# Decoder block on one core: where VectorE computes the convolution's 31 taps

## The chip, the cores and the metric

The kernel runs on one core of one Trainium2 chip. The metric is the device time of one execution in microseconds (us), the median of several runs; a second look comes from one profiled execution, whose span and rows are in us from its first instruction.

## The reference, cut to what matters

One decoder block on 256 tokens of width 1024, all in float32: a causal depthwise convolution branch and an attention branch run on the same projections, are gated and mixed, and a mixture of 32 experts (4 for each token) follows.

```python
u = rms_norm(h, norm1_g)
proj = u @ w_in                       # conv a, g (512 each), q, k, v (512 each), gates (2048)
# convolution branch
hc = a * sigmoid(g)
hc = depthwise_conv(hc, conv_dw, width 31, causal) + dw_b     # 512 channels
y_conv = silu(layer_norm(hc)) @ w_conv_out
# attention branch: 8 heads of 64, causal, ALiBi, q and k normed per head
y_attn = softmax(q k^T * scale - slope * distance) v @ w_attn_out
mixed = sigmoid(gate1) * y_conv + sigmoid(gate2) * y_attn
h = h + mixed @ w_out
u2 = rms_norm(h, norm2_g)
# top 4 of 32 experts, clamped SwiGLU, 2048-wide up/gate, 1024-wide down
h = h + moe_ffn(u2, w_router, w_up_gate, w_down, ...)
```

## The kernel before

The program is written by hand for each engine (`@block.sync`, `.scalar`, `.vector`, `.tensor`, `.gpsimd`); each engine executes its own list in order, and semaphores order the engines among one another. Nothing is scheduled by a tool: what stands ahead on an engine's list runs ahead.

**Dense stage.** The 1024x4608 projection is cut into nine groups of 512 columns: 0 and 1 are the convolution's two halves, 2, 3 and 4 are q, k and v, 5 to 8 are the gates. A dense product is made of three products (`product3`, L1038): every operand is split into a high part, rounded, and a low part, the difference. For weights, ScalarE writes the high part (`weights_high(i, b)`, L499, into `w_hi`) and VectorE the low part (`weights_low(i, b)`, L698, into `w_lo`), in two halves `b` for each group `i`. VectorE's `weights_low` waits for ScalarE's high part.

**Convolution.** The 31 taps are VectorE's (`taps(first, end)`). A round is one tap for all 512 channels: four instructions of 128x256, one for each block of 128 channels. Round 0 is at L720, the others at L723. A tap adds to the same accumulator `cv`, so each waits for the same channel block's tap of the round before. The last one raises `cv_done`. In the trace `hp` and `cv` are named `up_odd`, since they lie in the buffer of that expert's weights. Rounds 0 to 7 (`early_taps = 8`) stand ahead of the attention heads, among the low parts; the other 23 are dealt out over the eight heads, two or three to each:

```python
taps(*[early_taps + (TAPS - early_taps) * (h + i) // HEADS for i in range(2)])
```

**Attention on VectorE.** First `rqk` (L738) and the scaling of q and k (L744), then the four copies of q and k transposed (L752), then the loop over heads: a head adds the distance term to the scores (L766), takes the row maxima (L769, L770), their negative (L771, `nmx_ready`), then the reciprocal of the sums of the head before (L777, `rsm_ready`), then its taps; behind the taps of heads 2, 3, 5 and 7 stands a half of `weights_low(7)` or `weights_low(8)`, and behind those of heads 4, 6 a low part of the attention output (`attention_low`, L756).

**Attention on TensorE.** Groups 5 to 8 are 16 pieces of 24 matmuls (L1038); behind piece i stands `between(i)`: the transposes of q and k (L1130) at i = 1, the scores of head i-2 (L1103, L1104), the transposes of the probabilities of head i-5 (L1111), the product with v of head i-6 (L1121 to L1123), and at i = 11 the sum over channels for the convolution's layer norm (L1010), ahead of which TensorE waits for `cv_done`. The transposes of head g's probabilities need ScalarE's scaling, and that needs `rsm_ready` of head g, which VectorE raises in its piece for head g+1. The product with v of heads 2, 4 and 6 needs `attention_low` of the pair before.

**Behind it.** The layer norm, its sigmoid, the attention and convolution output products, mixing and `w_out` follow on the same chain, then the router, then one loop over tiles of tokens, expert by expert. The 32 experts' weights (12.6 MB each) stream through two sets of buffers, all on SyncE's queue. The first loads stand behind events of the dense stage: a part of expert 1's up weights behind `pv_done` of the last head, two behind the convolution's low part (`cv_lo`), others behind the mixing and `w_out`.

Of the kernel before, what the change touches and what calls it, by code (L numbers as in the profile page):

```python
# [56 lines left out]
def hybrid_block(nc, x, norm1_g, w_in, b_gates, conv_dw, conv_dw_b, conv_ln_g, conv_ln_b, w_conv_out,  # L57
# [3 lines left out]
    with ctx:  # L61
# [219 lines left out]
        def w_parts(i):  # L281
            k = stream[i][1].shape[1]
            return [t[:, :].rearrange("p (k n) -> p k n", k=k) for t in (w_hi[i % 2], w_lo[i % 3])]

        def half_cols(w, b):
            n = w.shape[2] // 2
            return w[:, :, b * n:(b + 1) * n]
# [371 lines left out]
        def _(dve):  # L659
            steps = [0]  # L660

            def done(ins):
                steps[0] += 1
                ins.then_inc(dve_step, 1)
                return steps[0]
# [29 lines left out]
            def weights_low(i, b):  # L695
                hi, lo = w_parts(i)
                dve.wait_ge(w_hi_ready, 2 * (i - 1) + b + 1)
                nc.vector.tensor_tensor(half_cols(lo, b), half_cols(stream[i][1], b), half_cols(hi, b).bitcast(F32),  # L698
                                        ALU.subtract).then_inc(w_lo_ready, 1)
# [15 lines left out]
            def taps(first, end):  # L715
                for w in range(first, end):
                    for c in range(KC):
                        tap = hp[:, c, w:w + T]
                        if w == 0:
                            landed[c] = done(nc.vector.tensor_scalar(cv[:, c, :], tap, dwT[:, c, 0:1], dwb[:, c:c + 1], ALU.mult, ALU.add))  # L720
                        else:
                            dve.wait_ge(dve_step, landed[c])
                            ins = nc.vector.scalar_tensor_tensor(cv[:, c, :], tap, dwT[:, c, w:w + 1], cv[:, c, :], ALU.mult, ALU.add)  # L723
                            if w == TAPS - 1 and c == KC - 1:
                                ins.then_inc(cv_done, 1)
                            else:
                                landed[c] = done(ins)

            early_taps = 8
            taps(0, 4)  # L730
            for b in range(2):
                weights_low(4, b)
            taps(4, early_taps)
            for b in range(2):
                weights_low(5, b)

# [4 lines left out]
            for i, t in enumerate((qn, kn)):  # L741
                v = t.rearrange("p m (h d) -> p (m h) d", d=HD)
                f = rqk[:, i * 16:i * 16 + 16].unsqueeze(2).to_broadcast([P, 16, HD])
                nc.vector.tensor_tensor(v, v, f, ALU.mult).then_inc(qk_scaled, 1)  # L744
            for b in range(2):
                weights_low(6, b)


            for j in range(4):
                i, m = divmod(j, 2)  # L750
                dve.wait_ge(qkT_full, j + 1)
                nc.vector.tensor_scalar((qT, kT)[i][:, :, m * P:(m + 1) * P], bank[4 + j][:].rearrange("p (a b) -> p a b", a=4),  # L752
                                        (qg, kg)[i], None, ALU.mult).then_inc(qkT_ready, 1)
            def attention_low(c):
                dve.wait_ge(o_hi, c + 1)
                nc.vector.tensor_tensor(ao_r[1][:, c, :], O_BANK[:, 0:T], ao_r[0][:, c, :].bitcast(F32), ALU.subtract).then_inc(o_read, 1)  # L756


            for h in range(HEADS + 1):
                if h < HEADS:  # L760
                    s = sc[h % 3]
                    slope = 2.0 ** (-8.0 * (h + 1) / HEADS)
                    dve.wait_ge(s_full, h + 1)
                    if h >= 3:
                        dve.wait_ge(t_full, h - 2)
                    nc.vector.scalar_tensor_tensor(s, dist, -slope * HD ** 0.5, S_BANKS[h % 2][:, 0:384],  # L766
                                                   ALU.mult, ALU.add).then_inc(s_read, 1)
                    dve.wait_ge(s_read, h + 1)
                    done(nc.vector.reduce_max(mx[:, h % 2, 0:1], s[:, 0:P], AX.X))  # L769
                    step(nc.vector.reduce_max(mx[:, h % 2, 1:2], s[:, P:3 * P], AX.X))  # L770
                    nc.vector.tensor_scalar(nmx[:, h % 2, :], mx[:, h % 2, :], -HD ** -0.5, None, ALU.mult).then_inc(nmx_ready, 1)  # L771
                if h >= 1:
                    g = h - 1
                    dve.wait_ge(exp_done, 2 * h)
                    if g >= 2:
                        dve.wait_ge(p_scaled, 2 * g - 2)
                    nc.vector.reciprocal(rsm[:, g % 2, :], sm[:, g % 2, :]).then_inc(rsm_ready, 1)  # L777
                if h < HEADS:
                    taps(*[early_taps + (TAPS - early_taps) * (h + i) // HEADS for i in range(2)])
                if h in (2, 3, 5, 7):  # L780
                    b = (2, 3, 5, 7).index(h)
                    weights_low(7 + b // 2, b % 2)
                if h >= 4 and h % 2 == 0:
                    attention_low((h - 4) // 2)
# [5 lines left out]
            freed(dve, U_MEAN)  # L790
            nc.vector.tensor_tensor(sq, xc, xc, ALU.mult).then_inc(sqr_ready, 1)
            attention_low(3)
            for b in range(2):
                weights_low(ATT_W, b)
# [598 lines left out]
```

## Time and profile before

| | us |
|---|---|
| median of 3 runs | 1136.68 |
| lowest, highest | 1135.35, 1137.06 |
| the profiled execution | 1133.76 |
| its span, first to last instruction | 1132.0 |
| TensorE busy in it | 970.9 |
| VectorE busy in it | 394.3 |
| ScalarE busy in it | 310.1 |
| HBM read | 431.59 MB |

The profiled execution lies 2.92 us below the median of the timed runs and 1.59 us below the lowest. In the rows a group of instructions is named by engine and line: PE is TensorE's matmuls, PEld its weight loads, DVE VectorE, ACT ScalarE, SPq SyncE's queue of transfers. The idle time in square brackets is that ahead of the instruction, with the engine and line whose work ended it. Two instructions of one engine can overlap by some 0.08 us in the rows, so what one more instruction costs is taken from start to start and not from the duration of one.

### The profile page before, as it was taken

The numbers are of one execution on the slowest core, as the hardware profiler recorded it, in microseconds if no ns is written. First come the engines' busy times: TensorE is split into PE (matmuls) and PEld (weight loads), VectorE is DVE, ScalarE is ACT, GpSimd is POOL, SyncE is SP. The second block draws the span as 40 slices with busy tenths as digits, with TensorE's granted clock in tenths as the row PEclk, the third lists the DMA queues.
The fourth block names the chain that finished last, engine by engine and source line by source line (L and its number), as shares of the span: only waits on it lengthen the run. The fifth ranks groups of instructions, "written<-read, shape, count | busy, mean of one in ns | idle before, by whom it ended". The sixth has DMA issues, their size and how long they took to land.

```text
span 1132.0 us, 19760 instructions
## 1 busy us (share of the span) xinstructions
PE 970.9 (86%) x7261; PEld 446.7 (39%) x7262; DVE 394.3 (35%) x1014; ACT 310.1 (27%) x534; POOL 5.3 (0%) x27
## 2 busy tenths in 40 slices
PE   6999698998766668889996799998997966998677
PEld 5998598732212113223331233332332321332122
DVE  4689968432111112222331133332332321232111
ACT  4565474122111111212222022331331311232111
POOL 1000000000000000000000000000000000000000
PEclk8999899999898888999998799999998999999888
DMA  7573068999999999999999999999999999999996
GB/s 268 178 278 138 12 223 354 402 406 425 426 430 426 426 426 427 426 426 426 426 426 426 426 426 426 426 425 424 427 426 426 427 426 426 426 428 426 426 427 252
DMA packets 50918, 432.97 MB, mean 382 GB/s; under 512 B 4845, under 2 KB 5265, under 8 KB 18128
## 3 DMA queue, kind: packets, MB, share of 16 engines
q1 hardware_dynamic: 50424, 432.50, 91.7%
q8 instruction: 16, 0.26, 0.1%
q10 hardware_dynamic: 472, 0.16, 0.1%
q14 instruction: 6, 0.05, 0.0%
HBM read 431.59 MB, written 1.05 MB: 382 GB/s over the span
## 4 chain that ended last, share of the span: by engine, by line
PE 48%; DMA 24%; SPq 20%; DVE 5%; issue 2%; ACT 1%; DVEq 0%; ACTq 0%
PE bank L1307 15%; SPq L404 12%; DMA up_odd<-in_w_up_gate 10%; DMA up_even<-in_w_up_gate 10%; PE bank L1038 9%; PE bank L1341 8%; SPq L410 6%; PE bank L1229 5%; DMA down_even<-in_w_down 3%; DVE up_odd L723 3%; PE bank L1298 3%; PE bank L1276 2%; PE bank L1068 1%; PE bank L1327 1%; DVE w_lo L698 1%
## 5 line engine op out<-in xcount | busy, mean ns | idle before, releaser
L1307 PE MATMUL bank<-up_even,reg_r 128*32 128x512 f32 x1472 | 187.2, 653 | 69.1 <-DMA up_even<-in_w_up_gate 69.1
L1307 PE MATMUL bank<-up_odd,reg_r 128*32 128x512 f32 x1408 | 186.2, 675 | 62.0 <-DMA up_odd<-in_w_up_gate 62.0
L993 DVE TENSOR_TENSOR ys<-reg_m,ys 64x512 fp32r<-64x512 f32 x90 | 61.7, 685 | 236.0 <-ACT ys L650 235.4
L1307 PEld LDWEIGHTS bank<-up_even,reg_r 128*32 128x32 f32 x1472 | 46.9, 115 | 202.0 <-DMA up_even<-in_w_up_gate 102.4
L1307 PEld LDWEIGHTS bank<-up_odd,reg_r 128*32 128x32 f32 x1408 | 45.6, 117 | 194.7 <-issue 97.4
L638 ACT ACTIVATE reg_m<-reg_m 128x256 f32<-128x256 f32 x45 | 18.9, 419 | 371.1 <-DVE reg_m L974 371.1
L1229 PE MATMUL bank<-reg_h,reg_r 128*32 128x256 f32 x736 | 93.2, 636 | 0.7 <-DVE reg_r L864 0.7
L974 DVE TENSOR_SCALAR reg_m<-bank 128x256 f32<-128x256 f32 x45 | 19.1, 425 | 212.4 <-PE bank L1307 212.4
L1341 PE MATMUL bank<-down_even,reg_r 128*32 128x512 f32 x736 | 84.4, 596 | 0.4 <-DMA down_even<-in_w_down 0.2
L646 ACT ACTIVATE reg_m<-bank,gslot 128x512 f32<-128x512 f32 x45 | 31.0, 688 | 194.8 <-PE bank L1341 194.8
L1341 PE MATMUL bank<-down_odd,reg_r 128*32 128x512 f32 x704 | 80.3, 595 | 0.1
L934 DVE TENSOR_TENSOR reg_r<-bank,g2c 128x256 f32<-128x256 f32 x46 | 19.5, 424 | 129.3 <-PE bank L1235 129.3
L638 ACT ACT_TABLE_LOAD x45 | 57.7, 1283 | 5.5 <-DVE cum L957 4.7
L650 ACT ACTIVATE ys<-reg_m 64x512 fp32r<-64x512 f32 x90 | 56.6, 629 | 2.0
L1298 PE MATMUL bank<-ys,hotT 128*128 128x512 f32 x184 | 56.9, 432 | 0.0
L630 ACT ACTIVATE reg_r<-bank 128x256 f32<-128x256 f32 x46 | 17.7, 384 | 131.7 <-PE bank L1229 131.7
L1298 PEld LDWEIGHTS bank<-ys,hotT 128*128 128x128 f32 x184 | 32.6, 198 | 51.2 <-issue 46.1
L723 DVE SCALAR_TENSOR_TENSOR up_odd<-up_odd,reg_m 128x256 f32<-128x256 f32 x120 | 48.3, 478 | 0.0
L1038 PE MATMUL bank<-u_hi,w_hi 128*128 128x256 f32 x160 | 48.2, 301 | 0.0
L1276 PE MATMUL bank<-bup,sel 128*128 128x512 f32 x92 | 47.2, 595 | 0.0
L1038 PE MATMUL bank<-u_lo,w_hi 128*128 128x256 f32 x160 | 46.4, 290 | 0.0
L1038 PE MATMUL bank<-u_hi,w_lo 128*128 128x256 f32 x160 | 46.3, 289 | 0.0
(252 smaller groups left out, 1185.7 us busy)
## 6 DMA issues: line engine op xcount, KB each, us to landing
up_even<-in_w_up_gate SPq DMA_DIRECT2D x64, 2048.0 KB, 36.4
up_odd<-in_w_up_gate SPq DMA_DIRECT2D x64, 2048.0 KB, 38.4
down_even<-in_w_down SPq DMA_DIRECT2D x64, 1024.0 KB, 36.5
down_odd<-in_w_down SPq DMA_DIRECT2D x64, 1024.0 KB, 36.5
down_even<-in_w_in SPq DMA_DIRECT2D x6, 2048.0 KB, 8.4
down_odd<-in_w_in SPq DMA_DIRECT2D x2, 2048.0 KB, 8.7
down_odd<-in_w_in SPq DMA_DIRECT2D x4, 512.0 KB, 8.9
down_odd<-in_w_attn_out SPq DMA_DIRECT2D x1, 2048.0 KB, 7.4
```

The lines of the kernel that those rows point to most:

```text
L404: sp.dma_start(up_part(a, c), w_up_gate[bass.ds(e, 1), :, :].rearrange("e (p k) n -> p (e k n)", k=KD)[:, n * c:n * c + n]).then_inc(up_in ...
L410: sp.dma_start(down_part(a, c), w_down[bass.ds(e, 1), 2 * c * P:(2 * c + 2) * P, :].rearrange("e (p r) n -> p (e r n)", r=2)).then_inc(dow ...
L638: nc.scalar.activation(ACT_B, ACT_A, ACT.Sigmoid, scale=ALPHA).then_inc(sigm_ready, 1)
L650: ins = nc.scalar.activation(ys[0:64, half, :], YR[r, :], ACT.Identity)
L723: ins = nc.vector.scalar_tensor_tensor(cv[:, c, :], tap, dwT[:, c, w:w + 1], cv[:, c, :], ALU.mult, ALU.add)
L993: ins = nc.vector.tensor_tensor(ys[64:P, half, :], YR[r, :], ys[0:64, half, :].bitcast(F32), ALU.subtract)
L1038: ins = mm(o, lhs(a, k), rhs(b, k), start=(k == 0 and i == 0), stop=(k == n - 1 and i == 2))
L1229: ins = mm(o[q * SLOTS:(q + 1) * SLOTS, 0:256].rearrange("s (k f) -> s k f", k=2), hot[:, m, :], features(m)[:, 2 * q:2 * q + 2, :], start ...
L1276: mm(UP[:], sel[:], bup[:], start=True, stop=False, skip_group_check=True)
L1298: ins = mm(acc[2 * m + half][:], hotT[:, m, :], ys[:, half, :], start=False, stop=False, skip_group_check=True)
L1307: ins = mm(UP[q * SLOTS:(q + 1) * SLOTS, :], XT[:, k % 2, k // 2 * SLOTS:(k // 2 + 1) * SLOTS], up_columns(a, k, q), start=False, stop=(k ...
L1341: ins = mm(YB[row:row + SLOTS, :], actT[:, j, c * SLOTS:(c + 1) * SLOTS], down[a][:, 2 * c + j, half * 512:(half + 1) * 512], start=(c == ...
```

## The change

The rounds of taps are dealt out anew. Before, rounds 0 to 3 stood ahead of the v group's low parts (`weights_low(4)`), 4 to 7 behind them. Now 0 to 4 stand ahead of them, round 5 between their two halves, 6 to 9 behind them; round 10 stands between the scaling of q and k and `weights_low(6)`, round 11 behind `weights_low(6)`, and round 12 behind the four copies of q and k transposed, ahead of head 0. `early_taps` is 13, so that 18 rounds are left for the heads. The rule in the loop gives 2, 2, 2, 3, 2, 2, 2, 3 rounds to heads 0 to 7; before it gave 2, 3, 3, 3, 3, 3, 3, 3. No instruction is added or taken away, and only VectorE's order differs.

```diff
-            early_taps = 8
-            taps(0, 4)
-            for b in range(2):
-                weights_low(4, b)
-            taps(4, early_taps)
+            early_taps = 13
+            taps(0, 5)
+            weights_low(4, 0)
+            taps(5, 6)
+            weights_low(4, 1)
+            taps(6, 10)
             for b in range(2):
                 weights_low(5, b)
...
                 nc.vector.tensor_tensor(v, v, f, ALU.mult).then_inc(qk_scaled, 1)
+            taps(10, 11)
             for b in range(2):
                 weights_low(6, b)
+            taps(11, 12)
...
                                         (qg, kg)[i], None, ALU.mult).then_inc(qkT_ready, 1)
+            taps(12, early_taps)
```

VectorE, from round 1 to the reciprocal of the q and k norms, before (`w_lo_50` belongs to the v group, `w_lo_51` to group 5, and L723 is a tap):

```order
L723 SCALAR_TENSOR_TENSOR up_odd<-up_odd,reg_m 128x256 x12
L698 TENSOR_TENSOR w_lo_50<-down_even,w_hi_52 128x8x256 x2
L723 SCALAR_TENSOR_TENSOR up_odd<-up_odd,reg_m 128x256 x16
L698 TENSOR_TENSOR w_lo_51<-down_even,w_hi_53 128x8x256 x2
L738 RECIPROCAL rqk<-rqk 128x32
```

The same place in the changed kernel:

```order
L723 SCALAR_TENSOR_TENSOR up_odd<-up_odd,reg_m 128x256 x16
L698 TENSOR_TENSOR w_lo_50<-down_even,w_hi_52 128x8x256
L723 SCALAR_TENSOR_TENSOR up_odd<-up_odd,reg_m 128x256 x4
L698 TENSOR_TENSOR w_lo_50<-down_even,w_hi_52 128x8x256
L723 SCALAR_TENSOR_TENSOR up_odd<-up_odd,reg_m 128x256 x16
L698 TENSOR_TENSOR w_lo_51<-down_even,w_hi_53 128x8x256 x2
L739 RECIPROCAL rqk<-rqk 128x32
```

Four taps more stand ahead of the v group's first low part and four between its two halves; the 16 behind it are as many as before.

VectorE, from the scaling of q and k to head 0's maxima, before (`w_lo_49` belongs to group 6, the copies from `bank` at L752 are q and k transposed, L766 takes head 0's scores):

```order
L744 TENSOR_TENSOR up_odd<-up_odd,rqk 128x1024 x2
L698 TENSOR_TENSOR w_lo_49<-down_odd,w_hi_52 128x8x256 x2
L752 TENSOR_SCALAR up_odd<-bank,par 128x4x128 x4
L766 SCALAR_TENSOR_TENSOR reg_r<-up_odd,bank 128x384
L769 TENSOR_REDUCE mx<-reg_r 128x1
```

In the changed kernel:

```order
L745 TENSOR_TENSOR up_odd<-up_odd,rqk 128x1024 x2
L723 SCALAR_TENSOR_TENSOR up_odd<-up_odd,reg_m 128x256 x4
L698 TENSOR_TENSOR w_lo_49<-down_odd,w_hi_52 128x8x256 x2
L723 SCALAR_TENSOR_TENSOR up_odd<-up_odd,reg_m 128x256 x4
L755 TENSOR_SCALAR up_odd<-bank,par 128x4x128 x4
L723 SCALAR_TENSOR_TENSOR up_odd<-up_odd,reg_m 128x256 x4
L771 SCALAR_TENSOR_TENSOR reg_r<-up_odd,bank 128x384
L774 TENSOR_REDUCE mx<-reg_r 128x1
```

Three blocks of four taps have come in, each ahead of work that another engine waits for.

VectorE, head 2 and the start of head 3, before:

```order
L766 SCALAR_TENSOR_TENSOR reg_r<-up_odd,bank 128x384
L769 TENSOR_REDUCE mx<-reg_r 128x1
L770 TENSOR_REDUCE mx<-reg_r 128x1
L771 TENSOR_SCALAR nmx<-mx 128x2
L777 RECIPROCAL rsm<-sm 128x2
L723 SCALAR_TENSOR_TENSOR up_odd<-up_odd,reg_m 128x256 x12
L698 TENSOR_TENSOR w_lo_50<-down_even,w_hi_53 128x8x256
```

In the changed kernel:

```order
L771 SCALAR_TENSOR_TENSOR reg_r<-up_odd,bank 128x384
L774 TENSOR_REDUCE mx<-reg_r 128x1
L775 TENSOR_REDUCE mx<-reg_r 128x1
L776 TENSOR_SCALAR nmx<-mx 128x2
L782 RECIPROCAL rsm<-sm 128x2
L723 SCALAR_TENSOR_TENSOR up_odd<-up_odd,reg_m 128x256 x8
L698 TENSOR_TENSOR w_lo_50<-down_even,w_hi_53 128x8x256
```

The head has eight taps where it had twelve; heads 1, 4, 5 and 6 lose four each in the same way, heads 0, 3 and 7 keep theirs.

## Rows read from the trace of the kernel before

**Rows 1.** The page: span, and HBM traffic in 40 slices of 28.3 us.

```profile
span 1132.0 us, 19760 instructions
...
GB/s 268 178 278 138 12 223 354 402 406 425 426 430 426 426 426 427 426 426 426 426 426 426 426 426 426 426 425 424 427 426 426 427 426 426 426 428 426 426 427 252
```

**Rows 2.** Windows: stretch, length; busy PE, PEld, DVE, ACT, POOL; TensorE clock; DMA share; GB/s.

```profile
45.00:87.00 42.00, 42.00 (x350) 41.53 (x348) 32.35 (x46) 25.56 (x81) 0.00 (x0) 1.00 0.65 239
92.00:142.00 50.00, 39.24 (x259) 34.03 (x258) 48.89 (x123) 23.45 (x64) 0.00 (x0) 0.90 0.21 83
...
175.00:232.00 57.00, 54.97 (x444) 46.09 (x448) 32.68 (x72) 16.63 (x28) 0.00 (x0) 1.00 0.99 406
262.00:1132.00 870.00, 733.19 (x5492) 247.69 (x5480) 222.16 (x691) 190.16 (x303) 0.00 (x0) 0.93 1.00 421
```

**Rows 3.** Chain of waits, 86 to 145 us: its shares, and its step behind the taps.

```profile
by line: DVE up_odd L723 53.8%; DVE w_lo L698 11.2%; PE bank L1038 5.6%; DVE reg_r L766 4.8%; issue 4.1%; DVE mx L770 3.4%; PE bank L1010 3.4%; DVE mx L769 2.9%; ACT L561 2.2%; DVE rsm L777 1.8%; ACT up_odd L544 1.4%; DVE ao_lo L756 1.1%; A
...
142.60 1.99 PE bank L1010 x8
```

**Rows 4.** VectorE's timeline, the heads: start, length, line, count.

```profile
87.02 0.56 DVE L766 SCALAR_TENSOR_TENSOR reg_r<-up_odd,bank 128x384 f32<-128x384 f32 x1 [2.29 <-PE bank L1104]
...
88.33 3.25 DVE L723 SCALAR_TENSOR_TENSOR up_odd<-up_odd,reg_m 128x256 f32<-128x256 f32 x8
91.50 0.55 DVE L766 SCALAR_TENSOR_TENSOR reg_r<-up_odd,bank 128x384 f32<-128x384 f32 x1
...
93.34 4.83 DVE L723 SCALAR_TENSOR_TENSOR up_odd<-up_odd,reg_m 128x256 f32<-128x256 f32 x12
98.08 0.55 DVE L766 SCALAR_TENSOR_TENSOR reg_r<-up_odd,bank 128x384 f32<-128x384 f32 x1
...
114.73 0.55 DVE L766 SCALAR_TENSOR_TENSOR reg_r<-up_odd,bank 128x384 f32<-128x384 f32 x1
...
137.72 4.82 DVE L723 SCALAR_TENSOR_TENSOR up_odd<-up_odd,reg_m 128x256 f32<-128x256 f32 x12
```

**Rows 5.** TensorE's waits from 92 to 142.6 us: sum, times, longest.

```profile
PE bank L1121 <- DVE ao_lo L756: 5.4, 2, 2.9
PE bank L1111 <- ACT up_odd L576: 4.4, 3, 2.1
PE bank L1103 <- DVE reg_r L766: 0.9, 1, 0.9
```

**Rows 6.** VectorE's timeline ahead of the heads.

```profile
47.17 4.84 DVE L723 SCALAR_TENSOR_TENSOR up_odd<-up_odd,reg_m 128x256 f32<-128x256 f32 x12
54.10 2.29 DVE L698 TENSOR_TENSOR w_lo<-down_even,w_hi 128x2048 fp32r<-128x2048 f32 x1 [2.09 <-ACT w_hi L499]
58.17 2.29 DVE L698 TENSOR_TENSOR w_lo<-down_even,w_hi 128x2048 fp32r<-128x2048 f32 x1 [1.78 <-ACT w_hi L499]
60.38 6.42 DVE L723 SCALAR_TENSOR_TENSOR up_odd<-up_odd,reg_m 128x256 f32<-128x256 f32 x16
...
72.28 2.36 DVE L744 TENSOR_TENSOR up_odd<-up_odd,rqk 128x1024 f32<-128x1024 f32 x2
75.97 4.58 DVE L698 TENSOR_TENSOR w_lo<-down_odd,w_hi 128x2048 fp32r<-128x2048 f32 x2 [1.33 <-ACT w_hi L499]
82.00 2.73 DVE L752 TENSOR_SCALAR up_odd<-bank,par 128x512 f32<-128x512 f32 x4 [1.45 <-PE bank L1130]
```

**Rows 7.** TensorE's timeline: head 0's scores, and head 3's transposes of probabilities.

```profile
86.06 0.48 PE L1103 MATMUL bank<-up_odd 64*128 64x128 f32 x2
...
118.36 0.52 PE L1111 MATMUL bank<-ident,reg_r 128*128 128x128 f32 x3 [2.10 <-ACT up_odd L576]
```

**Rows 8.** Windows, a stretch behind long waits of TensorE (columns as in rows 2).

```profile
121.50:126.50 5.00, 5.00 (x23) 4.67 (x24) 4.93 (x15) 2.05 (x7) 0.00 (x0) 0.50 0.00 0
```

**Rows 9.** SyncE's queue: the first loads of expert weights behind the heads.

```profile
155.21 0.35 SPq L348 DMA_DIRECT2D up_odd<-in_w_up_gate  x1
...
173.09 1.05 SPq L348 DMA_DIRECT2D up_odd<-in_w_up_gate  x2
```

## The prediction

> **What bounds the kernel now.** I read the page first. HBM traffic runs at 425 to 430 GB/s in nearly every slice from the tenth on, and almost nothing moves in the fifth slice (12 GB/s) [rows 1]. So the kernel has two parts: a dense stage that TensorE and VectorE set, and a long stream of expert weights that the DMA engines set. The windows say the same: from 262 us to the end the DMA share is 1.00 at 421 GB/s, and from 175 to 232 us it is 0.99 at 406 GB/s [rows 2]. Nothing that VectorE does faster inside the stream can pay. What can pay is to start the stream earlier, since it has to bring the same bytes whenever it starts.
>
> So I look at what sets its start. SyncE issues its loads in order, one of them behind the last head's product (155.21 us), two behind the convolution's low part (173.09 us) [rows 9]. Both hang on the stretch before. From 92 to 142 us VectorE is busy for 48.89 of 50 us, TensorE for 39.24 only, ScalarE for 23.45 [rows 2]. The chain of waits through 86 to 145 us is more than half taps (L723 53.8%), with the low parts of weights next (11.2%), and it enters TensorE at 142.60 us with L1010, the sum over channels that needs the last tap [rows 3]. So VectorE bounds the heads. Before the heads it doesn't: between 45 and 87 us TensorE is busy for all 42 us and VectorE for 32.35 [rows 2]. VectorE's rest lies in five waits that can be read one by one: 2.09 and 1.78 us for ScalarE's high parts of the v group, 1.33 us for those of group 6, 1.45 us for the transposes [rows 6], and 2.29 us for head 0's scores [rows 4].
>
> **The change, part by part.** *What a tap costs.* From start to start, head 1's twelve taps and their followers go from 93.34 to 98.08 us: 4.74 us for 12, 0.395 each. Head 0's eight go from 88.33 to 91.50 us, 3.17 us, 0.396 each [rows 4]. I take 0.396 us, so a round of four is 1.58 us. The duration in the rows overlaps with the next instruction and would overstate it.
>
> *Off the heads.* Heads 1, 2, 4, 5 and 6 lose one round each: 5 x 1.58 = 7.9 us. VectorE waits for next to nothing there, so its last tap of the heads, part of the block that starts at 137.72 us [rows 4], comes 7.9 us earlier, if no one else becomes late, and L1010 starts at 142.60 - 7.9 = 134.7 us.
>
> *Onto the front.* Each round must fit into a wait.
> First, the sixteen taps from 47.17 us end at 47.17 + 16 x 0.396 = 53.5 us; the high part is there for VectorE at 54.10 us [rows 6]: 0.6 us to spare. The low part ends, start to start, 2.2 us later (60.38 - 58.17 [rows 6]) at 56.3 us.
> Round 5 then takes it to 57.9 us, against 58.17 us [rows 6]: 0.3 us to spare. Behind that nothing differs up to q and k, as the sixteen taps from 60.38 us are as many as before.
> The scaling of q and k ends at 72.28 + 2.36 = 74.64 us [rows 6], the next can start at 74.56. Round 10 takes it to 76.1 us, where the low part started at 75.97 us: 0.15 us late. The two halves ran as one block of 4.58 us [rows 6], so the second high part was there in time, and they end at 80.5 us for the next to start. Round 11 takes it to 82.1 us; the copies started at 82.00 us [rows 6], so they are 0.1 us late and end at about 84.9 us. TensorE needs them for head 0's scores, which it reaches at 86.06 us [rows 7]: 1.2 us to spare. Round 12 starts at 84.8 us and ends at 86.4 us; head 0 starts on VectorE at 87.02 us [rows 4]: 0.6 us to spare. So all five rounds fit, and head 0 starts when it did. Cost of the front: 0 us. Bounds: at the least nothing, since head 0 waits for TensorE and can't start earlier; at the most, were each block of taps to cost its duration as read (6.42 us for 16, 0.401 each [rows 6]), 0.06 us more over the last twelve, still inside the 0.6 us. There is one more unseen thing, a gap of issue at the borders of the new blocks. For it I take 0 and keep up to 0.3 us each at two borders, less the slack of 0.6: again 0, so only the upper end of the range gets 0.3 us.
>
> The cover is thin, and it has a price: past the 0.6 us every further microsecond of front work starts head 0 late by one. No other engine waits for the moved low parts: group 6's are used behind head 1's scores, some 10 us later.
>
> The Trainium skill (VectorE: DVE Perf Modes, section on the TRN2 errata) gives a float32 two-input operation of N elements (N + 151)/0.96 ns, which is 424 ns for 256. By that, as an estimate, the moved rounds would be worth 20 x 0.424 = 8.5 us, and head 0 would still start in time. The rows' start to start disagrees, and the rows decide.
>
> *Who is late next.* TensorE had waits of 5.4 + 4.4 + 0.9 = 10.7 us from 92 to 142.6 us, all released by VectorE or by ScalarE behind VectorE [rows 5], which agrees with 50 - 39.24 = 10.8 us of idle time [rows 2]. 7.9 us of them go, about 2.8 us are left, so on the whole VectorE stays the bound. Place by place: head 3's transposes on TensorE started at 118.36 us [rows 7], 3.63 us behind head 4's start on VectorE at 114.73 us [rows 4]. Head 4 now starts two rounds earlier, 111.56 us, and the transposes can start at 115.2 us. TensorE still waits there, since it was waiting 2.10 us for them and another 0.9 us for the scores shortly before, and its own work starts no later than it did. The products with v of heads 2 and 4 wait for `attention_low`, which stands behind the taps, and so move with VectorE. ScalarE, busy less than half the time, has no wait that doesn't follow the other two.
>
> *Behind L1010.* The layer norm, output products, mixing, router and loads follow in the same order from 134.7 us. The transfers that they need have been issued by events that also move, or long before. So the load at 155.21 us goes out at about 147.3 us, the pair at 173.09 us at 165.2 us [rows 9]. From there the DMA engines are the bound, and each byte comes 7.9 us earlier.
>
> *Sum.* Span 1132.0 - 7.9 = 1124.1 us; the profiled execution's own time 1133.76 - 7.9 = 1125.9 us; against the median, which lies 2.92 us above that execution, 1136.68 - 7.9 = **1128.8 us**, 0.7% less. A measurement tells some 0.2% (2.3 us) from no change here.
>
> **The rivals.** *TensorE or its clock takes over part of the heads.* Behind its long waits TensorE ran at a granted clock of 0.50, the 1.2 GHz level, from 121.5 to 126.5 us [rows 8], and the mean over the heads was 0.90 [rows 2]. There, 24 matmuls took about 2 us more than at full clock. Five such pieces lie between 104 us and L1010. If all of them ran at the lower level, that is 10 us more work, of which two pieces' worth, one and a half really, was already paid: some 7 us more against 2.8 us of waits left, so 4 us of the gain would be lost: 1132.8 us. Against it: the waits get shorter, and the stretches with short waits ran at 1.00. 0.07.
>
> *The gain is swallowed by the stream.* If the weight stream were limited by something that doesn't start with the loads at 155 and 173 us, for example by a transfer already under way, the end would stay at 1136.7 us. Against it: 12 GB/s in the fifth slice [rows 1] and 83 GB/s over 92 to 142 us [rows 2] leave nothing under way. 0.05.
>
> *The stream is slower: the losing side.* The rate from 262 us on is 421 GB/s over 870 us [rows 2]. Each per cent of it costs 8.7 us. With the gain of 7.9 us, the kernel loses by more than 0.2% once the rate falls by (7.9 + 2.3)/8.7 = 1.2%, to 416 GB/s: at 1.5% less, 1136.7 - 7.9 + 13.1 = 1141.9 us. Place: all expert loads, whose start falls differently against TensorE's tiles. Against it: the order of loads and of tiles is the same, SyncE's queue holds several transfers, the slices hold 424 to 430 GB/s [rows 1], and the three runs lie within 1.7 us. 0.03.
>
> *The front overruns.* For the front to eat the gain, head 0 would have to start 7.9 us late, which with 0.6 us to spare and twelve taps behind the last fixed point means 0.396 + 8.5/12 = 1.1 us for a tap. The sixteen taps at 60.38 us took 0.40 us each at 239 GB/s of traffic [rows 2, 6]. 0.01, and in the middle case with it.
>
> **How the numbers follow.** The forecast, all five rounds off the path: 0.84, 1128.8 us. Part lost to TensorE: 0.07, around 1132.8 us. Swallowed: 0.05, 1136.7 us; the front's 0.01 goes to it. Slower: 0.03. The forecast's own range is 1127.2 to 1130.6 us: some 0.9 us for the scatter of a median of three, an idle stretch of 0.3 us that may go as well as come, and 0.3 us for issue gaps. The range to hold 8 in 10 reaches a little into the partial case: 1126.8 to 1131.8 us. Faster by over 0.2% means below 1134.4 us: 0.91; within 0.2%: 0.06; slower: 0.03.
>
> **What would show it.** In the profile of the changed kernel: VectorE's waits ahead of the heads should shrink from 2.09, 1.78, 1.33, 1.45 and 2.29 us to about 0.5, 0.2, 0, 0 and 0.6 us; head 0 should still start at 87.0 us, head 2 at 96.5 us; L1010 at 134.7 us; TensorE's waits over the heads should be about 3 us, with less time at 1.2 GHz; the last head's load at 147.3 us; and the stream's rate 421 GB/s as before. It would be wrong if head 0 starts later than 87.5 us, if TensorE's waits vanish and L1010 comes later than 136 us (it has become the bound), or if the loads go out 7.9 us earlier and the end doesn't.

## The result, and the profile after

| | us |
|---|---|
| before, median of 6 runs | 1136.07 |
| changed kernel, median of 6 runs (lowest, highest) | 1128.91 (1125.76, 1130.47) |
| ratio, 95% interval | 0.9933 [0.9915, 0.9951] |
| changed kernel, profiled execution | 1127.98 |
| its span | 1126.2 |

The change gains 7.2 us by the medians, 0.6 to 0.7%. Six more runs, beside those of the experiments, gave 1130.79 us against 1136.73, 5.9 us, with a ratio of 0.9939 [0.9921, 0.9957]. The ratios are estimated from all the runs of both kernels and are not the quotients of the medians, which are 0.9937 and 0.9948; all of these lie inside the intervals. Line numbers behind the edits are 1 to 5 higher in the changed kernel: L821, L1015, L1043 there are L816, L1010, L1038 of before.

VectorE's timeline ahead of the heads answers to [rows 6], and its last row but one to the first of [rows 4]:

```profile
54.57 2.29 DVE L698 TENSOR_TENSOR w_lo<-down_even,w_hi 128x2048 fp32r<-128x2048 f32 x1 [0.50 <-ACT w_hi L499]
56.78 1.67 DVE L723 SCALAR_TENSOR_TENSOR up_odd<-up_odd,reg_m 128x256 f32<-128x256 f32 x4
58.64 2.29 DVE L698 TENSOR_TENSOR w_lo<-down_even,w_hi 128x2048 fp32r<-128x2048 f32 x1 [0.19 <-ACT w_hi L499]
...
76.61 4.48 DVE L698 TENSOR_TENSOR w_lo<-down_odd,w_hi 128x2048 fp32r<-128x2048 f32 x2
...
82.60 2.72 DVE L755 TENSOR_SCALAR up_odd<-bank,par 128x512 f32<-128x512 f32 x4
85.23 1.66 DVE L723 SCALAR_TENSOR_TENSOR up_odd<-up_odd,reg_m 128x256 f32<-128x256 f32 x4
87.50 0.55 DVE L771 SCALAR_TENSOR_TENSOR reg_r<-up_odd,bank 128x384 f32<-128x384 f32 x1 [0.61 <-PE bank L1109]
...
96.98 0.55 DVE L771 SCALAR_TENSOR_TENSOR reg_r<-up_odd,bank 128x384 f32<-128x384 f32 x1
```

The five waits are 0.50, 0.19, 0, 0 and 0.61 us where they were 2.09, 1.78, 1.33, 1.45 and 2.29. Head 0 starts at 87.50 us, 0.48 later than before, but so does everything from the first tap on: round 0 starts at 46.36 us here and at 45.88 us before. From the first tap to head 0 it is 41.14 us in both.

TensorE's waits from 92 to 134.7 us, and its step into L1015, answer to [rows 5] and [rows 3]:

```profile
PE bank L1116 <- ACT up_odd L576: 1.9, 1, 1.9
PE bank L1126 <- DVE ao_lo L761: 1.7, 2, 1.0
```

```profile
134.81 1.99 PE L1015 MATMUL bank<-up_odd,reg_m 128*128 128x256 f32 x8 [1.80 <-DVE up_odd L723]
```

L1015 starts 7.79 us earlier than 142.60 us; counted from the first tap, 8.27 us earlier. TensorE still waits 1.80 us for the last tap: VectorE is still the bound of the heads.

Windows (columns as in [rows 2]), over the heads, over 5 us behind TensorE's wait for L821, and over the stream:

```profile
92.00:134.00 42.00, 37.41 (x264) 32.40 (x262) 41.16 (x104) 24.76 (x66) 0.00 (x0) 0.96 0.28 102
167.20:172.20 5.00, 5.00 (x29) 5.00 (x30) 5.00 (x5) 1.40 (x1) 0.00 (x0) 0.66 1.09 420
254.00:1124.00 870.00, 731.85 (x5512) 247.48 (x5504) 222.69 (x692) 192.10 (x306) 0.00 (x0) 0.93 1.00 421
```

SyncE's queue, the loads behind the last head, behind the convolution's low part, behind the mixing, and the first fetch of the expert loop; it answers to [rows 9]:

```profile
147.41 0.35 SPq L348 DMA_DIRECT2D up_odd<-in_w_up_gate  x1
...
165.29 1.05 SPq L348 DMA_DIRECT2D up_odd<-in_w_up_gate  x2
...
181.91 0.53 SPq L348 DMA_DIRECT2D up_odd<-in_w_up_gate  x1
...
224.60 4.86 SPq L404 DMA_DIRECT2D up_even<-in_w_up_gate  x4
```

The same queue before, for the last two:

```profile
188.23 0.33 SPq L348 DMA_DIRECT2D up_odd<-in_w_up_gate  x1
...
230.38 4.86 SPq L404 DMA_DIRECT2D up_even<-in_w_up_gate  x4
```

So the trace of after is 7.80 us ahead at the first two loads (155.21 and 173.09 before), only 6.32 us at the load behind the mixing, and 5.78 at the first fetch. The span ends 5.8 us earlier: behind the first fetch nothing differs. 1.5 us were lost between 165 and 182 us, and 0.5 us between 182 and 225 us. In the first place TensorE waits 2.3 us for L821 in both traces, but behind it the granted clock is 0.66 after and 1.00 before. Whether the change causes that was the first open question; whether the front is really free was the second.

### The profile page after: what moved, and what is told of

Same layout as the page of the kernel before. It is cut to its first block, busy times and chain, and to the rows that moved or that the text cites. A ratio compares the mean times of both kernels' runs of the same rounds, so it can differ in the third digit from the quotient of the medians.

```text
span 1126.2 us, 19760 instructions
## 1 busy us (share of the span) xinstructions
PE 967.3 (86%) x7261; PEld 445.8 (40%) x7262; DVE 393.8 (35%) x1014; ACT 309.8 (28%) x534; POOL 5.3 (0%) x27
## 4 chain that ended last, share of the span: by engine, by line
PE 48%; DMA 24%; SPq 20%; DVE 4%; issue 2%; ACT 1%; DVEq 0%; ACTq 0%
PE bank L1312 16%; SPq L404 12%; DMA up_odd<-in_w_up_gate 10%; DMA up_even<-in_w_up_gate 10%; PE bank L1043 9%; PE bank L1346 8%; SPq L410 6%; PE bank L1234 5%; DMA down_even<-in_w_down 3%; PE bank L1303 3%; PE bank L1281 2%; DVE up_odd L723 2%; PE bank L1073 1%; PE bank L1332 1%; DVE w_lo L698 1%
## 5 line engine op out<-in xcount | busy, mean ns | idle before, releaser
L1312 PE MATMUL bank<-up_even,reg_r 128*32 128x512 f32 x1472 | 189.9, 661 | 68.2 <-DMA up_even<-in_w_up_gate 68.2
L1312 PE MATMUL bank<-up_odd,reg_r 128*32 128x512 f32 x1408 | 179.4, 654 | 66.1 <-DMA up_odd<-in_w_up_gate 66.1
L723 DVE SCALAR_TENSOR_TENSOR up_odd<-up_odd,reg_m 128x256 f32<-128x256 f32 x120 | 48.6, 477 | 0.0
L1043 PE MATMUL bank<-u_hi,w_hi 128*128 128x256 f32 x160 | 47.2, 295 | 0.0
L1043 PE MATMUL bank<-w_hi,u_hi 128*128 128x256 f32 x160 | 45.5, 285 | 0.7 <-DVE u_lo L828 0.7
L1043 PE MATMUL bank<-u_lo,w_hi 128*128 128x256 f32 x160 | 45.6, 285 | 0.0
```

The lines of the kernel that those rows point to most:

```text
L1043: ins = mm(o, lhs(a, k), rhs(b, k), start=(k == 0 and i == 0), stop=(k == n - 1 and i == 2))
L1312: ins = mm(UP[q * SLOTS:(q + 1) * SLOTS, :], XT[:, k % 2, k // 2 * SLOTS:(k // 2 + 1) * SLOTS], up_columns(a, k, q), start=False, stop=(k ...
```

## The experiments

Every trace is read at the same events, counted from its own first tap (round 0, L720), which takes out whatever differs ahead of it: the first tap lies between 45.9 and 47.6 us. All in us; "mixing load" is the load behind the mixing (188.23 us before), "fetch" the first of the expert loop.

| kernel | head 0 | last-tap sum (L1010) | mixing load | fetch | end | ratio to before, 95% |
|---|---|---|---|---|---|---|
| before | 41.14 | 96.72 | 142.35 | 184.50 | 1086.1 | |
| before, again | 41.14 | 97.01 | 144.01 | 186.16 | 1087.9 | |
| changed | 41.14 | 88.45 | 135.55 | 178.24 | 1079.8 | 0.9933 [0.9915, 0.9951] |
| changed, again | 41.15 | 88.44 | 137.20 | 179.33 | 1081.5 | 0.9939 [0.9921, 0.9957] |
| heads alone | 41.14 | 88.79 | 135.90 | * | * | 1.0063 * |
| front alone | 41.14 | 96.72 | 143.85 | 186.00 | * | 1.0069 * |
| block of 13 | 43.94 | 92.75 | 139.88 | 182.51 | 1084.1 | 0.9966 [0.9950, 0.9981] |
| 15 early | 43.63 | 87.30 | 134.39 | 176.54 | 1077.9 | 0.9906 [0.9878, 0.9934] |
| 11 early | 41.14 | 91.62 | 140.39 | 182.54 | 1083.6 | 0.9960 [0.9945, 0.9974] |
| mix before low part | 41.15 | 88.46 | 133.64 | 175.79 | 1080.3 | 0.9919 [0.9902, 0.9937] |
| one round with the heads | 41.14 | 81.33 | 126.86 | * | * | 0.9872 * |
| group 8 last, mix before low | 41.15 | 86.25 | 131.44 | 175.01 | 1076.8 | 0.9910 [0.9896, 0.9924] |
| group 8 last | 41.15 | 86.26 | 133.37 | 175.52 | 1076.5 | 0.9892 [0.9878, 0.9907] |
| all three | 43.61 | 86.17 | 131.25 | 175.35 | 1076.9 | 0.9891 [0.9877, 0.9905] |

The three kernels marked * compute another convolution, so the router picks other experts, and the loop has more tiles of tokens: one row for each tile's first step, of the page of "before" and of "heads alone":

```profile
L974 DVE TENSOR_SCALAR reg_m<-bank 128x256 f32<-128x256 f32 x45 | 19.1, 425 | 212.4 <-PE bank L1307 212.4
```

```profile
L974 DVE TENSOR_SCALAR reg_m<-bank 128x256 f32<-128x256 f32 x47 | 20.0, 425 | 184.4 <-PE bank L1307 184.4
```

45 tiles against 47 (47 and 48 in the other two). Their times from end to end say nothing of the taps; their events ahead of the router do.

### Each half alone

```diff
 # heads alone (edit of the kernel before: rounds 8 to 12 left out)
-taps(*[early_taps + (TAPS - early_taps) * (h + i) // HEADS for i in range(2)])
+taps(*[13 + (TAPS - 13) * (h + i) // HEADS for i in range(2)])
 # front alone (edit of the changed kernel: rounds 8 to 12 done twice)
-taps(*[early_taps + (TAPS - early_taps) * (h + i) // HEADS for i in range(2)])
+taps(*[8 + (TAPS - 8) * (h + i) // HEADS for i in range(2)])
```

> Half of the change: the heads have 18 rounds of taps dealt out as in the changed kernel, and the front has only its 8 rounds in the old places; rounds 8 to 12 are left out, so the convolution misses five of its 31 taps. Theory (the gain is 5 rounds of 1.58 us off VectorE in the heads, and the front's rounds cost nothing): the same time as the changed kernel, 0.993 of before, L1010 at 134.7 +- 0.3 us against 142.60, head 0 at 87.0 to 87.5 us with a wait of 2.3 us ahead of it. Rival (the front's new rounds cost something although head 0 starts on time, for instance by slowing ScalarE or TensorE beside them): faster than the changed kernel by more than 1 us, 0.992 or less.

> The other half: the front has 13 rounds as in the changed kernel, and the heads still have 23, so that rounds 8 to 12 are done twice and the convolution's sum is wrong by them. Theory: the time of before, ratio 1.000 +- 0.001, head 0 at 87.0 to 87.5 us, L1010 at 142.6 us +- 0.5. Rival (the front costs): slower by 1 us or more, ratio 1.001 to 1.003. Rival (order in the front itself helps, as low parts come closer to their use): faster, 0.998 or less.

Measured, VectorE's first tap and TensorE's sum with the front alone, and that sum with the heads alone:

```profile
46.92 1.38 DVE L720 TENSOR_SCALAR up_odd<-up_odd,reg_m,par 128x256 f32<-128x256 f32 x4
```

```profile
143.64 1.99 PE L1015 MATMUL bank<-up_odd,reg_m 128*128 128x256 f32 x8 [0.30 <-DVE up_odd L723]
```

```profile
134.72 1.99 PE L1010 MATMUL bank<-up_odd,reg_m 128*128 128x256 f32 x8 [1.57 <-DVE up_odd L723]
```

With the front alone the sum comes 96.72 us behind the first tap, as before to the hundredth: the five rounds in the waits cost nothing. With the heads alone it comes 7.93 us earlier, five rounds of 1.59 us. The forecasts of the ratios were misses, since neither had thought of the router; the events decide. The front alone also has 47.1 us from the sum to the mixing load (143.85 - 96.72), the same as the changed kernel, with the heads' order of before. So the 1.5 us don't come from the heads' shorter waits.

The changed kernel's sum comes another 0.34 us earlier than that of the heads alone. VectorE's rows show where. Ahead of a reciprocal in the heads it stands idle for 0.27 us in which the profile shows nothing that it waited for:

```profile
131.18 0.17 DVE L777 RECIPROCAL rsm<-sm 128x2 f32<-128x2 f32 x1 [0.27 <-issue]
```

This stretch is there in both traces of before, with the heads alone (0.26 us) and with the front alone, and in none of the other ten traces. Why it is there isn't known.

### Is the lost 1.5 us the change's?

> The kernel before, unchanged, for a second trace. Its first trace had TensorE at clock 1.00 behind the wait of 2.4 us for the attention output's mixing (L816), and 45.6 us from L1010 to the load behind the mixing; the changed kernel had 0.66 and 47.1 us. Theory (that drop comes or not from run to run, whatever the order of taps): 45.6 or 47.1 us, and L1010 at 96.7 us from the first tap again. Rival (the change causes the drop, through its shorter waits in the heads): 45.6 us. Seven traces of other kernels with that wait have 47.1 us or more, so 47.1 is the likelier.

> The changed kernel, unchanged, for a second trace and more runs beside those of its relatives. Theory: ratio to before 0.9931 to 0.994; L1010 at 88.5 us from the first tap against 96.7; 47.1 us from L1010 to the load behind the mixing in most runs, 45.6 in the rest. Rival (the trace of before was the usual one and the change really gives 1.5 us back behind the heads): the ratio stays at 0.9945 or above.

The same 5 us behind the wait for L816 in the second trace of before:

```profile
177.00:182.00 5.00, 5.00 (x30) 5.00 (x31) 5.00 (x5) 1.31 (x1) 0.00 (x0) 0.66 1.09 421
```

The kernel before has the drop too: 0.66, and 47.0 us from the sum to the mixing load where its first trace had 45.6. So the 1.5 us are not the change's; how often each kernel pays them can't be told from two traces of each. Of the eleven traces that keep the wait of 2.3 us, two escape the drop behind it: the first of before, and that with one round with the heads (45.5 us). The changed kernel's second trace loses another 1.65 us between the sum and the last head's load (14.25 us, against 12.60 in the first), again with clock 0.66 over 135 to 140 us, behind the 1.80 us wait for the last tap. The trace of "11 early" has the same loss there (14.26 us), while the four others that have a wait of 1.6 to 1.8 us at this place run on at 1.00. Between the second traces the gain up to the sum is 97.01 - 88.44 = 8.57 us, up to the fetch 6.83 us, at the end 6.4 us; the ratio of 0.9939 is what was expected, but its interval also takes in the rival's 0.9945, so it is the events that decide.

This is what the Trainium skill says (TensorE: Matmul & The Clock Gate, part on the HAM clock gate): full clock is granted for activity and withdrawn when the array idles, and the moment differs from run to run. The rows agree: a wait of 2.3 us was followed by 0.66 over the next 5 us in one trace of the kernel before and by 1.00 in the other.

### The places in the front

```diff
 # edit of the kernel before
-early_taps = 8
+early_taps = 13
```

> The whole change in number but not in place: 13 rounds early, put in the two old places (4 ahead of the v group's low parts, 9 behind them), heads as in the changed kernel. Theory (a round is free only inside a wait): the block of 9 rounds pushes group 5's low parts by 7.9 us, behind it lie waits of 0.69, 1.33, 1.45 and 2.29 us, 5.8 in all, so head 0 starts 2.1 us later on VectorE; TensorE also waits 1 us or so for group 5's low part at 75.8 us. L1010 at 136.8 to 137.9 us, 2.1 to 3.2 us behind the changed kernel, ratio to before 0.9955. Rival (the places don't matter, only the numbers): L1010 at 134.8 us, 0.993.

Measured, VectorE's timeline, TensorE's waits from 60 to 92 us, and VectorE's from 88 to 139 us:

```profile
60.65 14.34 DVE L723 SCALAR_TENSOR_TENSOR up_odd<-up_odd,reg_m 128x256 f32<-128x256 f32 x36
74.89 4.50 DVE L698 TENSOR_TENSOR w_lo<-down_even,w_hi 128x2048 fp32r<-128x2048 f32 x2
...
90.10 0.56 DVE L766 SCALAR_TENSOR_TENSOR reg_r<-up_odd,bank 128x384 f32<-128x384 f32 x1 [1.01 <-PE bank L1104]
```

```profile
PE bank L1103 <- DVE up_odd L752: 1.3, 1, 1.3
PE bank L1038 <- DVE w_lo L698: 1.2, 1, 1.2
```

```profile
DVE reg_r L766 <- PE bank L1104: 1.9, 2, 1.0
DVE rsm L777 <- ACT reg_r L563: 0.9, 1, 0.9
```

The same counts in the old places give half of the gain (0.9966). Head 0 is 2.80 us late, and the sum 4.3 us later than in the changed kernel, more than the 2.1 to 3.2 expected. The block delays low parts and q and k, so TensorE waits 2.5 us, and being late itself it then holds VectorE up at heads 0 and 1, and ScalarE at head 1's reciprocal: 2.8 us of waits on VectorE, where the changed kernel has 0.61 and 0.36. The effect was expected in kind, but its expected size was too small.

### How many rounds

```diff
 # 15 early: edit of the changed kernel
-early_taps = 13
+early_taps = 15
 # 11 early: edit of the changed kernel
-early_taps = 13
+early_taps = 11
...
-taps(11, 12)
...
-taps(12, early_taps)
```

> Two rounds more ahead of head 0 than in the changed kernel: 15 early and 16 with the heads, two to each. Theory (the slack ahead of head 0 is 0.6 us, behind it each round costs what it saves): head 0 starts 2 x 1.58 - 0.61 = 2.55 us later, the heads save 3.17 us, L1010 comes 0.6 us earlier than in the changed kernel, unless TensorE becomes the bound; ratio to before 0.9925. Rival (head 0's start isn't what sets the pace, the sum of taps in the heads is): L1010 3.2 us earlier, 0.9905. Rival (a late head 0 costs fully and TensorE bounds the heads): L1010 2 us later, 0.995.

> Three of the five rounds moved: 11 early, in the places of the changed kernel up to the one behind the scaling of q and k, 20 with the heads. Theory (each round off the heads is worth 1.58 us on its own): L1010 3.2 us later than in the changed kernel, at 137.9 to 138 us, ratio to before 0.9958. Rival (the gain comes only once the last rounds go, as TensorE's waits and its lower clock in the heads vanish together): 0.998 or more, or L1010 later than 139.5 us.

With 11 early the sum comes at 91.62 us from the first tap, 3.17 us later than with 13: two rounds of 1.585 us. From 8 to 11 early it is 5.10 us, three such rounds and the idle stretch. So each round has the same price, and neither TensorE's clock nor a joint effect of the last rounds is needed to explain it. With 15 early, head 0 is 2.49 us late (2.55 expected) and the sum 1.15 us earlier than with 13, where 0.6 was expected. Most of the remaining 0.5 us is a second wait of the changed kernel, at head 1, which the count had left out:

```profile
93.74 0.17 DVE L782 RECIPROCAL rsm<-sm 128x2 f32<-128x2 f32 x1 [0.36 <-ACT reg_r L563]
```

With 15 early this wait is gone, as VectorE gets there later. From end to end the ratio is 0.9906, and its interval overlaps that of the changed kernel.

> The changed kernel without rounds 13 to 29: the heads have one round, the last, with head 7, and 17 rounds of taps are left out. It asks where TensorE or ScalarE takes over. Theory: VectorE has 17 x 1.58 = 26.9 us less to do in the heads, but TensorE's own work from 104.6 us to L1010 takes 26 us at full clock, so L1010 comes at 130 to 131 us, only 4 us earlier than in the changed kernel, with TensorE's waits near zero; ratio to before 0.989. Rival (VectorE's other work and ScalarE still pace the heads): L1010 at 133 us or later. Rival (no limit near): L1010 before 125 us.

```diff
 # edit of the changed kernel: rounds 13 to 29 left out
-taps(*[early_taps + (TAPS - early_taps) * (h + i) // HEADS for i in range(2)])
+taps(*((13, 13) if h < HEADS - 1 else (TAPS - 1, TAPS)))
```

Windows, the heads of that kernel:

```profile
92.00:128.40 36.40, 36.40 (x268) 31.85 (x268) 20.94 (x46) 24.52 (x66) 0.00 (x0) 1.00 0.33 116
```

TensorE never waits and stays at 1.00, and the sum comes 7.1 us earlier than in the changed kernel (4 expected). Behind the point that the expectation counted from, TensorE's own work took some 23 us and not 26. The 26 us had been read from a trace that ran partly at the lower clock; from the mean of 0.96 over its 42.7 us that accounts for some 1.7 us (an estimate), and the rest isn't explained. So the heads have 7.1 us left in them before TensorE is the bound throughout.

### The order behind the heads, and group 8's low parts

```diff
 # mix before low part: edit of the changed kernel
-weights_low(CONV_W, 1)                 # behind cv_lo
 for b in range(4):                     # attention output times gate, L821
     ...
+weights_low(CONV_W, 1)
 # group 8 last: edit of the changed kernel, in the loop over heads
-if h in (2, 3, 5, 7):
-    b = (2, 3, 5, 7).index(h)
-    weights_low(7 + b // 2, b % 2)
+if h in (2, 3):
+    weights_low(7, h - 2)
+if h == HEADS:                         # behind head 7's reciprocal
+    for b in range(2):
+        weights_low(8, b)
```

> The changed kernel with the second half of the convolution weights' low part moved behind the four products of attention output and gate (L821), so that TensorE finds its bank free 2.2 us earlier. Theory (the dense chain moves the stream one for one; and TensorE's 2.3 us wait there can drop its clock, which cost 1.5 us in the profiled run of the changed kernel): the wait of 2.3 us goes down to some 0.1 us, the stretch of 5 us behind it runs at clock 1.00 and not 0.66, the load behind mixing goes out 2.2 to 3.7 us earlier, the whole is 2.2 to 3.7 us faster than the changed kernel, ratio to before 0.990 to 0.9915. Rival (from the loads at 165 us on the DMA engines alone set the end): no faster than the changed kernel, 0.993.

> The kernel of the run before last but two (product with the gate ahead of the low part), and group 8's two low parts moved from behind the taps of heads 5 and 7 to behind the reciprocal of head 7. Theory (VectorE still bounds the heads, TensorE has some 3.6 us of waits left there and 1.8 us ahead of L1010): VectorE's last tap 2.2 us earlier, L1010 1.8 us earlier, at 133.0 us, then TensorE has no wait left ahead of it; with the other edit 4 to 5.5 us faster than the changed kernel, ratio to before 0.988 to 0.9895. Rival (TensorE already bounds): nothing beyond what the gate edit alone gives. Rival (the low parts are now late for group 8): a wait at TensorE's piece 12 or 14 and a loss of 1 us or more against the gate edit alone.

> The changed kernel with group 8's low parts behind head 7's reciprocal, and without the edit at the mixing. It splits the earlier combined run. Theory: L1010 2.2 us earlier than in the changed kernel, 86.3 us from the first tap, as in the combined run, and 47.1 us behind it; ratio to before 0.9915 (7.2 + 2.2 us). Rival (the earlier last tap is given back behind the heads): 0.993.

> All that helped: product with the gate ahead of the low part, group 8's low parts behind head 7's reciprocal, and 15 rounds early. Theory: VectorE bounds the heads still, but TensorE has 2.9 us of waits left for heads 3 and 2 and 0.3 us ahead of L1010, so the two rounds more give the 0.6 to 1.1 us that they gave without the other edits, L1010 at 85.2 to 85.7 us from the first tap, ratio to before 0.990. Rival (TensorE is the bound now and a late head 0 only hurts): L1010 at 86.5 us or later, 0.9915.

With the gate's product first, the stretch behind it runs at full clock:

```profile
168.00:173.00 5.00, 5.00 (x44) 5.00 (x43) 5.00 (x3) 1.34 (x1) 0.00 (x0) 1.00 1.09 420
```

From the sum to the mixing load it is 45.2 us instead of 47.1. That is 1.9 us, less than the 2.2 to 3.7 us expected, although both the wait of 2.3 us and the drop behind it are gone. TensorE now waits for VectorE further on, at the mixing:

```profile
PE bank L1043 <- DVE u_lo L828: 1.8, 2, 0.9
```

In the changed kernel VectorE had itself waited twice 0.86 us for TensorE there; here it works without a pause through the mixing and is the bound. The fetch comes 2.45 us earlier than in the changed kernel's first trace, 0.5 us of it because that trace had lost 0.5 us between the mixing load and the fetch. The whole is 0.9919 where at most 0.9915 was expected, and its profiled execution gained nothing, the span being 1127.4 us. The loss sits in the loop's last tile. Its product with the last up weights begins at 1102.37 us in this trace and at 1102.32 us in that of "group 8 last"; TensorE's timeline of the two, from there:

```profile
1102.37 3.64 PE L1312 MATMUL bank<-up_odd,reg_r 128*32 128x512 f32 x16 [1.75 <-DMA up_odd<-in_w_up_gate]
1105.94 2.08 PE L1303 MATMUL bank<-ys,hotT 128*128 128x512 f32 x4
```

```profile
1102.32 1.92 PE L1314 MATMUL bank<-up_odd,reg_r 128*32 128x512 f32 x16 [1.53 <-DMA up_odd<-in_w_up_gate]
1104.17 1.20 PE L1305 MATMUL bank<-ys,hotT 128*128 128x512 f32 x4
...
1112.44 1.07 PE L1348 MATMUL bank<-down_odd,reg_r 128*32 128x512 f32 x8 [0.32 <-DMA down_odd<-in_w_down]
```

The same matmuls take 3.64 and 1.92 us. From there to the end it is 25.0 us here and 21.2 us there, at a mean granted clock of 0.70 and 0.96; the first traces of before and after took 22.1 us each. Transfers still cover some of this in the first 10 us, as the last down weights are landing: in "group 8 last" TensorE waits for them at 1112.44 us. Behind them nothing does, and TensorE's next step, at 1115.74 and 1113.43 us, is 2.3 us apart; what follows adds 1.6 us. So part of the scatter of this kernel, up to some 4 us, lies in its last tile, and it goes with the clock there.

"Group 8 last" moves the sum 2.2 us forward, as expected, and is the fastest together with "all three": 0.9892 and 0.9891, 12 us less than before, 5 us less than the changed kernel by the ratios, and more than the 0.9915 expected. From the first tap to the end its trace is 3.3 us shorter than the changed kernel's first and 5.0 us shorter than its second. For that pair of traces the events account for the whole: of the 5.0 us, 3.8 lie ahead of the fetch, 0.5 in the last tile, whose clock was 0.96 (21.2 against 21.7 us), and 0.7 in the stream between. Only 2.2 us of them are gained at the sum; 1.65 us are the drop ahead of the last head's load, which the second trace had and the first had not. Whether the medians differ for the same reasons isn't shown.

The combinations gave less than their sum: "group 8 last, mix before low" has 0.9910 where 0.988 to 0.9895 was expected. With group 8 last, the gate edit still wins 1.9 us up to the mixing load, but the way from there to the fetch is 43.57 and 44.10 us long in the two kernels that have both, against 42.15 in most traces. In both the clock there is 0.87, behind the two waits of 0.9 us at the mixing; "mix before low part" has the same two waits and 42.15 us. In "all three":

```profile
177.00:190.00 13.00, 12.05 (x87) 11.85 (x88) 7.54 (x7) 6.44 (x7) 0.00 (x0) 0.87 1.01 422
```

And the two further rounds of "all three" give 0.08 us at the sum instead of 0.6 to 1.1: TensorE no longer waits ahead of it. VectorE's last tap comes 1.2 us earlier by the two rounds, but TensorE, which is busy without a wait from 118.10 us on, isn't there before 133.05 us. In this kernel it is the bound at the end of the heads.

## Why the prediction was right, point by point

- *VectorE bounds the heads, not the front*: right. The sum over channels follows the number of rounds in the heads at 1.58 to 1.59 us each (five off in "heads alone", two between 13 and 11 early), while the same rounds in the front cost 0.00 us. The five waits listed are 8.9 us of VectorE's rest; a sixth, 0.69 us ahead of group 5's second low part, was passed over and wasn't needed.
- *Off the heads, 7.9 us*: right, 7.93 us with the heads alone, 8.27 and 8.57 us between traces of the two kernels. The excess of 0.3 us fits the idle stretch of 0.27 us, which the prediction had left open and which the changed kernel doesn't have; in the second pair another 0.3 us comes in, as TensorE and not the last tap was late at the sum before.
- *Onto the front, 0*: right, with waits left as worked out: about 0.5, 0.2, 0, 0 and 0.6 us forecast, 0.50, 0.19, 0, 0 and 0.61 measured.
- *The cover is thin, and past it a microsecond costs one*: right for head 0 with two rounds more (2.49 us late against 2.55), though the sum lost less, as a wait of 0.36 us at head 1 went too. The same count put without regard to the waits cost more than one for one, since TensorE became late as well.
- *TensorE keeps 2.8 us of waits*: 5.4 us, the 3.6 us above and 1.80 us ahead of the sum. The step took TensorE's own work as fixed, but with shorter waits it ran less at the lower clock (0.96 against 0.90 over the heads) and was busy for 37.4 us instead of 39.2, which left more waits. The mistake was on the safe side.
- *The loads at 147.3 and 165.2 us*: 147.41 and 165.29. That they fit to 0.1 us is partly luck: the first tap was 0.48 us late in this trace and the idle stretch gave 0.34 us back. For the same reason the sign "head 0 later than 87.5 us" was badly chosen, as it isn't counted from a common event: head 0 starts at 87.50 us here and at 88.67 us in the second trace, 41.14 and 41.15 us behind the first tap.
- *Behind that everything follows one for one*: right for the order of work, wrong in size for a single trace. TensorE's clock behind two waits took 1.5 and 0.5 us of the gain in the profiled run, and the first tap was 0.48 us late; 8.27 less these is 5.78 us, the measured shift of the fetch. Both kernels pay such drops, and the medians differ by 7.2 us (0.9933) and 5.9 us (0.9939); what share of the missing 0.7 to 2 us is drops and what is the scatter of medians isn't shown. The rival on TensorE's clock was wrong for the heads, where the clock rose. The drops that cost time lie behind the heads, where no wait hides them, and they aren't the change's.
- *The stream is rigid*: right. From the fetch to the end it is 901.6 us in both, at 421 GB/s over the same length.
- *1128.8 us*: 1128.91. The mechanism holds, but the fit to 0.1 us is luck: the median of before was 0.6 us lower over six runs than over the three that the forecast started from, and the gain was 0.7 us smaller than 7.9. The second set, 1130.79 us, lies inside the range to hold 8 in 10 and 0.2 us above the forecast's own.

## What to carry to other kernels

Read the idle time ahead of single instructions on the engine that bounds the next stage: work that has no due time can be cut to fit into each wait, and its price is then zero as long as the next fixed event isn't late. The same work in one block beside the waits can cost half of what it brings. When a prologue feeds a saturated stream, a microsecond of the prologue is a microsecond of the whole; and when an experiment leaves work out ahead of a router, compare events ahead of the router, not ends.

## What the runs showed of the hardware

- A wait of TensorE of 2.3 us was followed by a stretch at the lower level of its clock (mean 0.66 over 5 us) in nine of eleven traces, and not in the other two; of the kernel before, one trace has it and one has not. Waits of 1.6 to 1.8 us ahead of the sum were followed by it in two of six traces. It costs 1.4 to 1.7 us each time that TensorE is the bound.
- The clock also differs in the last tile of the stream: 21.2 us at a mean of 0.96 and 25.0 us at 0.70, from the product with the last up weights to the end; most traces lie at 21.7 to 22.1 us.
- The weight stream itself hardly scatters: 900.9 to 902.2 us from the first fetch to the end in ten traces of kernels with 45 tiles; only the one with the slow last tile had 904.5.
